# An expert's rows gathered by TensorE in transposed form

## The reference

```python
xf = rmsnorm(h, norm_ffn_g)                        # 256 x 2048
probs = softmax(xf @ router_w)                     # 16 experts in 4 groups
# best group by its two best experts, and those two experts; weights gw sum to 1
for e in range(16):
    rows = tokens that chose e                     # padded blocks
    hid  = silu(xf[rows] @ w_gate[e]) * (xf[rows] @ w_up[e])    # 2048 -> 1024
    out[rows] += gw[rows, e] * (hid @ w_down[e])                # 1024 -> 2048
```

## Time and profile before

| | |
|---|---|
| median of three runs | 1223.97 us |
| profiled execution, its own time | 1226.38 us |
| its span | 1224.6 us |
| TensorE busy, products / weight loads | 1148.5 us (94%) / 527.1 us (43%) |
| VectorE, ScalarE, GpSimd busy | 386.1, 118.6, 8.7 us |
| mean granted TensorE clock | 0.987 |
| DMA over the span | 460.71 MB, 376 GB/s |

### The profile page before, as it was taken

The page is one execution under the profiler, slowest core; times in us unless marked ns, Lnnn a source line. Parts: engine busy times, 40 slices in busy tenths (PEclk is TensorE's granted clock), DMA queues, the critical chain, the costliest instruction groups (busy, mean ns, idle before and its releaser), DMA issues.

```text
span 1224.6 us, 12049 instructions
## 1 busy us (share of the span) xinstructions
PE 1148.5 (94%) x5201; PEld 527.1 (43%) x5201; DVE 386.1 (32%) x581; ACT 118.6 (10%) x202; POOL 8.7 (1%) x24
## 2 busy tenths in 40 slices
PE   7999999999999999999989898989989898989886
PEld 6888888887333333333323232323233332322222
DVE  6866787776222111111211111111111111111113
ACT  1303002011020000000000000000010000000002
POOL 0200000000000000000000000000000000000000
PEclk9999999999999999999999999999999999999998
DMA  9856544597999999999999999999999999999993
GB/s 347 303 201 202 199 171 146 190 426 311 374 389 434 430 429 433 430 434 428 432 431 430 431 432 433 430 429 432 432 432 431 429 430 435 432 431 428 431 427 157
DMA packets 32880, 460.71 MB, mean 376 GB/s; under 512 B 4136, under 2 KB 5696, under 8 KB 19264
## 3 DMA queue, kind: packets, MB, share of 16 engines
q1 hardware_dynamic: 32832, 459.98, 90.1%
HBM read 457.87 MB, written 2.10 MB: 376 GB/s over the span
## 4 chain that ended last, share of the span: by engine, by line
PE 61%; DMA 36%; DVE 1%; ACT 1%; issue 0%; DVEq 0%; SPq 0%
PE bank L1142 25%; DMA blocks<-in_moe_w_gate 23%; DMA blocks<-in_moe_w_up 10%; PE bank L969 7%; PE bank L971 7%; PE bank L970 7%; PE bank L1198 6%; PE bank L1121 3%; PE bank L1101 2%; DMA late<-in_moe_w_gate 2%; DMA late<-in_moe_w_up 2%; PE bank L1110 1%; PE bank L1014 1%; PE bank L943 1%; DMA blocks<-in_a_w_in 0%
## 5 line engine op out<-in xcount | busy, mean ns | idle before, releaser
L856 DVE TENSOR_TENSOR acc<-acc,bank 128x512 f32<-128x512 f32 x128 | 82.2, 684 | 461.9 <-PE bank L1121 461.9
L1142 PE MATMUL bank<-blocks,xg_a 128*64 128x512 f32 x832 | 199.7, 624 | 24.5 <-DMA blocks<-in_moe_w_gate 22.3
L1198 PE MATMUL bank<-blocks,sil 128*64 128x512 f32 x864 | 190.6, 595 | 13.2 <-DMA blocks<-in_moe_w_down 12.5
L1142 PE MATMUL bank<-blocks,xg_b 128*64 128x512 f32 x752 | 167.9, 599 | 5.9 <-DMA blocks<-in_moe_w_up 4.4
L1142 PEld LDWEIGHTS bank<-blocks,xg_a 128*64 128x64 f32 x832 | 60.1, 142 | 157.6 <-issue 148.3
L635 DVE TENSOR_TENSOR w_lo<-blocks,w_hi 128x1024 fp32r<-128x1024 f32 x96 | 117.7, 1226 | 3.3
L1198 PEld LDWEIGHTS bank<-blocks,sil 128*64 128x64 f32 x864 | 60.1, 137 | 133.6 <-issue 110.8
L1142 PEld LDWEIGHTS bank<-blocks,xg_b 128*64 128x64 f32 x752 | 53.0, 138 | 117.7 <-issue 103.4
L882 DVE TENSOR_TENSOR sil<-sil,bank 64x512 f32<-64x512 f32 x16 | 11.1, 692 | 262.2 <-ACT sil L566 262.2
L633 DVE CAST w_hi<-blocks 128x1024 fp32r<-128x1024 f32 x96 | 67.1, 699 | 62.2 <-PE bank L971 61.5
L969 PE MATMUL bank<-w_hi,act_first 128*128 128x512 f32 x192 | 77.1, 402 | 0.8 <-DVE act_first L650 0.8
(11 more groups left out here) (174 smaller groups left out, 691.7 us busy)
## 6 DMA issues: line engine op xcount, KB each, us to landing
blocks<-in_moe_w_down SPq DMA_DIRECT2D x25, 4096.0 KB, 38.9
blocks<-in_moe_w_up SPq DMA_DIRECT2D x23, 4096.0 KB, 40.2
blocks<-in_moe_w_gate SPq DMA_DIRECT2D x22, 4096.0 KB, 39.4
blocks<-in_a_w_in SPq DMA_DIRECT2D x31, 1024.0 KB, 5.5
late<-in_moe_w_up SPq DMA_DIRECT2D x7, 4096.0 KB, 39.8
late<-in_moe_w_gate SPq DMA_DIRECT2D x7, 4096.0 KB, 40.2
blocks<-in_a_w_out SPq DMA_DIRECT2D x16, 1024.0 KB, 5.2
late<-in_moe_w_down SPq DMA_DIRECT2D x4, 4096.0 KB, 40.7
```

The source lines that it names most:

```text
L856: V.tensor_tensor(acc[:, b, cols], acc[:, b, cols], bank[5 + j % 3][:, :], ALU.add)\
L1142: ins = T.matmul(bank[c][at:at + TOK, :], xg(unit // 4 * 8 + unit % 2 * 4 + s), weights[:, s * F + c * BANK:s * F + (c + 1) * BANK], start ...
L1198: ins = T.matmul(bank[2 + c // 2][at:at + TOK, :], hidden, weights[:, s * D + c * BANK:s * D + (c + 1) * BANK], start=(j == 0 and s == 0), ...
```

## The change

The gather's operands change places. x becomes the left, stationary operand: 128 tokens by 128 features, every 8th column of a 1024-column piece (`every(8, ...)`), and `pick` the right, moving one with its 64 columns. Output: partition = feature, free = place, 64 columns for each of the eight feature groups (s, h) of a bank. This is the layout that the transposes left, so `take_half` reads the bank directly. The copies of rows on ScalarE and VectorE, `transpose_rows` and their three semaphores are gone. A gather has 16 products in place of 4, and x is read in both versions as fp32.

```diff
-        x_row = y[:, 0, :]
...
-        row_a_ready = sem("row_a_ready")
-        row_b_ready = sem("row_b_ready")
-        row_transposed = sem("row_transposed")
...
@@ ScalarE, once before the items and then in each item
-            act.wait_ge(gathered, 1)
-            nc.scalar.copy(x_row, bank[6][:, :]).then_inc(row_a_ready, 1)
...
-                if not last:
-                    act.wait_ge(gathered, i * 2 + 3)
-                    nc.scalar.copy(x_row, bank[6][:, :]).then_inc(row_a_ready, 1)
...
@@ VectorE
             def take_half(n, g):
-                dve.wait_ge(row_transposed, 2 * n + (g + 1))
+                dve.wait_ge(gathered, 2 * n + (g + 1))
...
-            def take_second_row(n):
-                dve.wait_ge(gathered, n * 2 + 2)
-                dve.wait_ge(row_transposed, n * 2 + 1)
-                V.tensor_copy(x_row, bank[7][:, :]).then_inc(row_b_ready, 1)
...
-                    take_second_row(i + 1)
                     take_half(i + 1, 0)
                     take_half(i + 1, 1)
-            take_second_row(0)
             take_half(0, 1)
...
@@ TensorE
-            def columns_of(cols, h):
-                return cols.rearrange("p (n h s) -> p n h s", h=2, s=4)[:, :, h, :]
             def gather(jj):
-                for b in range(NB):
+                for s in range(4):
                     for h in range(2):
-                        last = T.matmul(bank[6 + jj][h * TOK:(h + 1) * TOK, :], pick[:, b, :],
-                                        columns_of(x[:, b, jj * PIECE:(jj + 1) * PIECE], h),
-                                        start=(b == 0), stop=(b == NB - 1))
+                        at = (2 * s + h) * TOK
+                        for b in range(NB):
+                            rows = every(8, x[:, b, jj * PIECE:(jj + 1) * PIECE], 4 * h + s)
+                            last = T.matmul(bank[6 + jj][:, at:at + TOK], rows, pick[:, b, :],
+                                            start=(b == 0), stop=(b == NB - 1))
                 last.then_inc(gathered, 1)
-            def transpose_rows(n, jj):
-                pe.wait_ge((row_a_ready, row_b_ready)[jj], n + 1)
-                for s in range(4):
-                    last = T.transpose(bank[6 + jj][:, s * P:(s + 1) * P], every(4, x_row, s), ident[:, :])
-                last.then_inc(row_transposed, 1)
...
             gather(0)
             keep_warm(4, 3)
-            transpose_rows(0, 0)
             keep_warm(4, 5)
...
                     gate_or_up(unit)
-                    if first and unit == 1:
-                        transpose_rows(0, 1)
...
                 if not last:
                     gather(1)
-                    transpose_rows(i + 1, 0)
                 pe.wait_ge(hid_ready, i + 1)
                 for f in range(4):
                     ins = T.transpose(bank[4][:, f * P:(f + 1) * P],
                                       every(4, hid[:, :], f), ident[:, :])
                 ins.then_inc(hid_transposed, 1)
-                if not last:
-                    transpose_rows(i + 1, 1)
```

## The result

| | before | after |
|---|---|---|
| median | 1224.45 us (1223.38 to 1227.46, 4 runs) | 1410.07 us (1409.32 to 1410.73, 4 runs) |
| ratio | | 1.1508, 95% interval 1.1487 to 1.1528 |
| profiled span | 1224.6 us | 1408.9 us |
| mean granted clock | 0.987 | 0.901 |

A forecast was written before the change was run, and what follows sets the result against it. Weight loads by DMA were taken to bound the kernel, with TensorE counting only before 338.8 us. Changes of +1.3, +2.4, -0.7 and +2.1 us there gave 1223.97 + 5.1 = 1229.1 us, range 1226 to 1244.

The forecast's parts named there:

- The bound and the rule: Expert stages: weight loads set the end; a TensorE microsecond added before 338.8 us costs one, later ones are hidden.
- The pitch of the new gather: Time per record of the new gather's products: 120 ns, so 3.84 us for a gather's 32 records.
- the upper end: Highest pitch considered for the gather's loads: 179 ns, from 106 ns plain streaming plus 73 ns for the stride.
- the strided surplus: Extra time of a strided over a contiguous transpose load, 212 - 139 = 73 ns, added for the upper end.
- The line rule of the Trainium skill: SBUF has 16-byte lines, a new line at each access is penalised; so columns 8 apart cost the same as 4.
- The sum A to D: TensorE path up to 338.79 us: start +1.3, item 0's second gather +2.4, transposes -0.7, next item's gather +2.1; +5.1 us.
- Rival 1: Later items: TensorE overtakes DMA above 57.2 us an item, pitch from 141 ns; 1250 us at 160, 1271 at 180; 12%.
- Rival 2: Clock falls to 1.2 GHz around the gathers, 1.79 us a fall: 1238 us once per item, 1267 after both gathers; 8%.
- Wait for hid_t, silu under the gather: Behind the second gather: silu chain hidden, wait for hid_t open inside 1.36 us before the down products.
- the copies are worth nothing: Removing one 128x512 copy each on ACT and DVE per item, under 0.7 us, gains nothing behind 339 us.
- rival 3: Gather: loads as fast as contiguous transpose loads, pitch about 55 ns, so not slower: -1.1 us, 1222.9 us; 8%.
- Rival 4: DMA gap at 337 us not TensorE's doing or made good later: +0 to +2 us, 1225 us; 8%.

The follow-up runs named there:

- experiment 8: Kernel before the change, with 20 more warming products ahead of unit 0 of item 0: 1230.76 us, ratio 1.0030.
- experiment 9: Kernel before the change, with 12 warming products behind the second gather in each item from 1 on: 1228.18 us, ratio 1.0015.
- experiment 10: Kernel before the change, item 0's second gather issued ahead of unit 0 in place of the eight warming products: 1225.40 us, ratio 1.0004.
- experiment 11: As experiment 10, and in item 0 the next item's first gather moved behind unit 7, ScalarE's row copy behind the silus: 1224.04 us, ratio 0.9990.
- experiment 2: Changed kernel, gather reading every 4th column of x (16 bytes apart) in place of every 8th: 1407.97 us, ratio 1.1477.
- experiment 4: Changed kernel, gather reading every 2nd column of x (8 bytes apart) in place of every 8th: 1234.06 us.
- experiment 5: Changed kernel, gather reading every 16th column of x (64 bytes apart) in place of every 8th: 1372.97 us.
- experiment 6: Kernel before the change, row transposes reading every 8th column (32 bytes apart) in place of every 4th: 1226.78 us.
- experiment 7: Kernel before the change, row transposes reading every 2nd column (8 bytes apart) in place of every 4th: 1226.52 us.
- experiment 1: Changed kernel, each gather product reading 128 neighbouring columns of x in place of every 8th: 1233.07 us, ratio 1.0051 to the kernel before.
- experiment 3: Changed kernel, same loads of every 8th column but 128 moving columns in place of 64: 1334.34 us, ratio 1.0870 to the kernel before.

## Why the prediction was wrong

- **The bound and the rule** (weights set the end; TensorE counts ahead of 339 us only) were right for time added to the kernel before, up to 55 us an item: experiments 8 and 9. For time saved, experiments 10 and 11 don't bear them out.
- **The pitch of the new gather was wrong**, the step "I take 120 ns: it is the only strided row, and the plain stream (106) fits under it". It is 238 to 244 ns, above the upper end too (179). The row was of a transposing load. The forecast's other reason, that the plain stream fits under it, took the plain stream at its contiguous speed. The rows held a warning, which I used as a number to add: contiguous, the plain load streams at half the transposing one's speed (106 against 55). Adding the strided surplus gave 179; doubling the strided transposing load (128) would have given 256, close to what came. Experiments 2 and 4 to 7 show that no rule of that kind is safe either. The line rule of the Trainium skill was weighed, but only to say that 32 bytes cost what 16 do, which is nearly so (335 and 329 ns a load); what 16 bytes cost this load I took from the other kind.
- **The sum A to D** was right in itself: at the pitch of 110 ns experiment 1 gives 4.1 us by rows, as the formula does.
- **Rival 1** (TensorE becomes the bound from 141 ns on, 1.02 us per ns behind it) had the mechanism and the price: at 240 ns it gives 5.1 + 0.096 x 21 = 7.1 up to its start at 141 ns, and 1.02 x 99 = 101 from there, +108 us. Experiment 3, with these loads and the full clock, measured +106.6 (1334.34 less 1227.74). It had 12% and was priced only to 180 ns.
- **Rival 2** (the clock) came together with rival 1, which the prediction didn't provide for: it stood as an alternative beside gathers of 3.84 us. Slow loads and few moving columns together caused it: with 64 columns moving under loads of 110 and 116 ns the clock stayed at 1.00 in the early items (experiments 1 and 4), under 217 to 240 ns it fell, and with 128 columns under 240 ns it stayed. The price was 1.79 us a fall, 3.6 for an item's two; they cost 5.0.
- **Wait for hid_t, silu under the gather**: about as forecast. From the gather's end to the down products it is 1.1 us in experiment 3 and 1.2 in experiment 1, where the forecast had 1.36, and 1.53 with the slow clock (366.89 to 368.42). That the copies are worth nothing fits experiment 1's item of 55.2 us; no run takes them alone.
- **Rivals 3 and 4**: rival 3 needed a pitch near 55 ns, and even contiguous loads had 110 (experiment 1). Rival 4 needed the added time to be hidden, and in experiment 8 it wasn't.
- **The range** was built from the forecast's neighbours although an unmeasured operation stood in the path 1024 times. Where the price of such an operation has only relatives in the trace, the range has to reach as far as it would with the dearest relative and the two rivals together.

## What to carry to other kernels

Swapping the operands to get a transposed result can put a strided read on the stationary operand. Here it put one at 32 bytes under 64 records an item, where the old kernel had moved x in runs of four columns and had, for the same work, strided stationary loads only in eight row transposes. Before such a swap, count how often the load will run and how far its columns are apart. An fp32 left operand of 128x128 in a plain product cost 0.22 to 0.24 us a record here when read at 16 bytes or more, and 0.11 to 0.12 at 4 or 8 bytes. A product with few moving columns under a slow load cost twice here: for itself, and through the clock for what comes behind it.

## What was not expected of the hardware

- Stationary fp32 loads of 128x128, the load's record: plain 192 ns at 4 bytes, 197 at 8, 329 at 16, 335 at 32, 311 at 64; transposing 139 at 4, 209 at 8, 209 to 212 at 16, 192 at 32. Plain, the pitch goes from 110 ns at 4 bytes to 238 at 32.
- The granted clock fell to 1.2 GHz with TensorE busy for 99% of the time and without a wait ahead of it, inside gathers of 32 loads with 64 moving columns each, and stayed at 2.4 GHz with 128 moving columns under the same loads.
- The slow loads took 335 ns at the full clock and 336 ns at half of it.
